# Small weight columns in sixteen parts behind later loads, and FoX's first keys ahead of GLA's first queries and keys

## What is computed

```
h = rms_norm(x, g_norm1) * (1.0 + scale1) + shift1
proj = h @ w_in                       # (256, 2048) @ (2048, 16416)
(gq, gk, gv, gg, ga_low, fq, fk, fv, f_logit, gate_a, gate_b) = split(proj)
log_a = log_sigmoid(ga_low @ w_gla_a_up + b_gla_a) / GLA_TAU   # ga_low: 16 columns
log_f = log_sigmoid(f_logit + b_fox_f)                         # f_logit: 16 columns
```

## Time and profile before

| | |
|---|---|
| median of three runs | 1872.38 us (1868.65 to 1874.75) |
| the profiled execution | 1868.97 us |
| its span, first to last instruction | 1867.2 us |
| TensorE busy | 1825.2 us (98%) |
| VectorE / ScalarE busy | 1251.1 us (67%) / 852.0 us (46%) |
| mean granted TensorE clock | 0.994 |
| moved by DMA | 445.71 MB, mean 239 GB/s |

### The profile page before, as it was taken

The page is one execution under the profiler, slowest core; times in us unless marked ns, Lnnn a source line. Parts: engine busy times, 40 slices in busy tenths (PEclk is TensorE's granted clock), DMA queues, the critical chain, the costliest instruction groups (busy, mean ns, idle before and its releaser), DMA issues.

```text
span 1867.2 us, 21786 instructions
## 1 busy us (share of the span) xinstructions
PE 1825.2 (98%) x8353; PEld 1482.5 (79%) x8353; DVE 1251.1 (67%) x1402; ACT 852.0 (46%) x1089; POOL 21.2 (1%) x44
## 2 busy tenths in 40 slices
PE   6998999999999999999999999999999999999998
PEld 3666888888888888888887788788888888888886
DVE  5997667676666667667666787876555555555555
ACT  4444555455544544334433455443444344434443
POOL 1000000000000000000000000000000000000000
PEclk9999999999999999999999999999999999999999
DMA  9998898899987987999989786687665666666663
GB/s 383 401 320 256 217 225 280 244 238 254 210 211 241 214 240 242 254 263 323 323 241 272 258 284 217 220 277 230 193 188 181 197 190 188 188 195 191 182 191 125
DMA packets 216944, 445.71 MB, mean 239 GB/s; under 512 B 18565, under 2 KB 35045, under 8 KB 216458
## 3 DMA queue, kind: packets, MB, share of 16 engines
q1 hardware_dynamic: 215448, 440.77, 78.7%
q10 hardware_dynamic: 1138, 3.50, 0.5%
q0 software_dynamic: 256, 0.05, 0.0%
HBM read 442.12 MB, written 2.10 MB: 238 GB/s over the span
## 4 chain that ended last, share of the span: by engine, by line
PE 81%; DMA 6%; DVE 3%; issue 2%; ACT 1%; SPq 1%; POOLq 0%; POOL 0%; DVEq 0%; ACTq 0%
PE ps L1815 75%; DMA raw<-in_w_in 4%; DMA raw<-in_w_proj_fox 1%; PE ps L1799 1%; ACT whi L714 1%; DVE wlo L1193 1%; DMA raw<-in_w_proj_gla 1%; DVE acc L1311 1%; PE ps L1919 1%; SPq L597 0%; DVE acch L1165 0%; PE ps L1971 0%; PE ps L1725 0%; PE ps L1928 0%; PE ps L1723 0%
## 5 line engine op out<-in xcount | busy, mean ns | idle before, releaser
L1193 DVE TENSOR_TENSOR wlo<-raw,whi 128x1024 fp32r<-128x1024 f32 x604 | 738.1, 1224 | 559.5 <-ACT whi L714 557.4
L714 ACT ACTIVATE whi<-raw 128x1024 fp32r<-128x1024 f32 x604 | 639.4, 1060 | 917.7 <-PE ps L1815 663.6
L1815 PE MATMUL ps<-whi,hT 128*128 128x512 f32 x3264 | 1042.5, 395 | 7.9 <-DVE wlo L1193 7.6
L1815 PEld LDWEIGHTS ps<-whi,hT 128*128 128x128 f32 x3264 | 615.3, 189 | 154.8 <-DVE wlo L1193 16.7
L1815 PE MATMUL ps<-wlo,hT 128*128 128x512 f32 x1632 | 637.4, 391 | 0.0
L1815 PE MATMUL ps<-whi,oaT 128*128 128x512 f32 x1248 | 390.9, 392 | 0.0
L1815 PEld LDWEIGHTS ps<-wlo,hT 128*128 128x128 f32 x1632 | 308.0, 189 | 63.2 <-issue 1.9
L1815 PEld LDWEIGHTS ps<-whi,oaT 128*128 128x128 f32 x1248 | 234.4, 188 | 49.6 <-issue 1.2
L1815 PE MATMUL ps<-wlo,oaT 128*128 128x512 f32 x624 | 243.0, 389 | 0.0
L1311 DVE SCALAR_TENSOR_TENSOR acc<-raw,cond,acc 128x1024 f32<-128x1024 f32 x120 | 153.4, 1278 | 0.2
L1815 PEld LDWEIGHTS ps<-wlo,oaT 128*128 128x128 f32 x624 | 117.2, 188 | 25.1 <-issue 1.2
(11 more groups left out here) (245 smaller groups left out, 817.6 us busy)
## 6 DMA issues: line engine op xcount, KB each, us to landing
raw<-in_w_ff SPq DMA_DIRECT2D x264, 512.0 KB, 4.0
raw<-in_w_in SPq DMA_DIRECT2D x248, 512.0 KB, 7.0
raw<-in_w_ada SPq DMA_DIRECT2D x128, 512.0 KB, 5.8
first<-in_w_ada SPq DMA_DIRECT2D x64, 512.0 KB, 10.2
raw<-in_w_in SPq DMA_DIRECT2D x64, 256.0 KB, 6.2
raw<-in_w_proj_fox SPq DMA_DIRECT2D x32, 512.0 KB, 5.8
raw<-in_w_proj_gla SPq DMA_DIRECT2D x32, 512.0 KB, 5.6
raw<-in_w_out SPq DMA_DIRECT2D x32, 512.0 KB, 4.9
```

Of the source, the lines that this page charges most:

```text
L714: nc.scalar.activation(parts(g)[0][:], raw[POS_G[g] % RING][:], ACT.Copy).then_inc(s_hi, 1)
L1193: V.tensor_tensor(rest[:], raw[POS_G[g] % RING][:], top[:].bitcast(F32), ALU.subtract).then_inc(s_lo, 1)
L1815: i = T.matmul(ps[bank(name, t)][:], src[:, kt, hl, tk], w[:, k, :], start=(kt == 0 and n == 0), stop=(kt == KT - 1 and n == 2))
```

## The change

Four things are edited. The two sections behind HEAD change places: `fk0` has units 24 to 31, `qk0` units 32 to 39, and their stage, turn and take change places with them. The two small DMAs become sixteen: behind each of the loads at stream positions 30 to 37 stand two that bring 2 of the 16 row blocks (256 runs of 64 bytes, 16 KB, each). `small_hi` waits for all sixteen. And the chain of the small columns is written one to three steps later; `shift_sum` stays where it was.

```
-FOX = [("qk", 0), ("fk", 0), ("fv", 0)] + ...
+FOX = [("fk", 0), ("qk", 0), ("fv", 0)] + ...
+SMALL_FROM = G_FOX + 6
...
             for pos in range(loaded, len(STREAM)):
-                if pos == G_FOX + 4:
+                load(pos)
+                if SMALL_FROM <= pos < SMALL_FROM + UG:
                     sp.wait_ge(s_zero, 1)
-                    sp.dma_start(small[:, :, 0:RANK], w_in_v[:, :, C_LOW:C_LOW + RANK]).then_inc(s_small, 16)
-                    sp.dma_start(small[:, :, 32:32 + FH], w_in_v[:, :, C_FL:C_FL + FH]).then_inc(s_small, 16)
-                load(pos)
+                    ks = slice(KU * (pos - SMALL_FROM), KU * (pos - SMALL_FROM) + KU)
+                    sp.dma_start(small[:, ks, 0:RANK], w_in_v[:, ks, C_LOW:C_LOW + RANK]).then_inc(s_small, 16)
+                    sp.dma_start(small[:, ks, 32:32 + FH], w_in_v[:, ks, C_FL:C_FL + FH]).then_inc(s_small, 16)
...
-                act.wait_ge(s_small, 32)
+                act.wait_ge(s_small, 32 * UG)
```

ScalarE's steps (stage and take of `fk0` and `qk0` change places as well):

```
-                    if u == 8:
+                    if u == 11:
                         small_hi()
-                    if u == 12:
+                    if u == 14:
                         small_log()
-                    if u == 13:
+                    if u == 15:
                         decay_abs()
-                    if u == 14:
+                    if u == 16:
                         logs()
-                    if u == 21:
+                    if u == 22:
                         decay_evac()
```

More of the change, by code:

```diff
@@ L39 @@
 HEAD = [("gg", 0), ("gv", 0), ("fq", 0)]
-FOX = [("qk", 0), ("fk", 0), ("fv", 0)] + [(what, it) for it in range(1, 4) for what in ("fq", "fk", "fv")]
+FOX = [("fk", 0), ("qk", 0), ("fv", 0)] + [(what, it) for it in range(1, 4) for what in ("fq", "fk", "fv")]
 GLA = [(what, it) for it in range(1, 4) for what in ("qk", "gg", "gv")]
@@ L756, in fox_stage @@
                 if u == 8:
-                    stage(("fq", it) if it else ("qk", 0), fqk_tok)
+                    stage(("fq", it) if it else ("fk", 0), fqk_tok)
                 if u == 11:
@@ L762, in fox_stage @@
                     else:
+                        take_turned(("fk", 0), ((fk, 1.0),))
+                if u == 16:
+                    stage(("fk", it) if it else ("qk", 0), fqk_tok)
+                if u == 19:
+                    if it:
+                        take_turned(("fk", it), ((fk, 1.0),))
+                    else:
                         take_turned(("qk", 0), ((gq[0], GSC), (gk[0], 1.0)))
[L764 to L767, removed]
             def shift_silu(g):
@@ L1499, in _ @@
                     else:
-                        if u == 8:
+                        if u == 11:
                             small_lo()
-                        if u == 11:
+                        if u == 13:
                             small_join()
-                        if u == 13:
+                        if u == 15:
                             decay_min()
-                        if u == 14:
+                        if u == 16:
                             log_sigmoids()
-                        if u == 16:
+                        if u == 17:
                             forget_cols()
-                        if u == 18:
+                        if u == 19:
                             forget_cums()
@@ L2007, in _ @@
                     else:
-                        if u == 11:
+                        if u == 13:
                             small_cols()
-                        if u == 13:
+                        if u == 15:
                             decay_logits()
-                        if u == 16:
+                        if u == 17:
                             forget_turn()
-                        if u == 18:
+                        if u == 19:
                             forget_sums()
-                        if u == 20:
+                        if u == 21:
                             decay_sums()
@@ L2020, in _ @@
                     if u == 10:
-                        turn(("fq", it) if it else ("qk", 0), fqk_tok)
+                        turn(("fq", it) if it else ("fk", 0), fqk_tok)
                     if u == 18:
-                        turn(("fk", it), fqk_tok)
+                        turn(("fk", it) if it else ("qk", 0), fqk_tok)
                     if u < 8:
@@ L2026, in _ @@
                         if it or u >= FOX_EARLY:
-                            token_unit(("fq", it) if it else ("qk", 0), u, hT, ready)
+                            token_unit(("fq", it) if it else ("fk", 0), u, hT, ready)
                     elif u < 16:
-                        token_unit(("fk", it), u - 8, hT)
+                        token_unit(("fk", it) if it else ("qk", 0), u - 8, hT)
                     else:
```

## The result

| | before | after |
|---|---|---|
| median (lowest to highest) | 1870.52 us (1866.81 to 1874.75), 4 runs | 1885.38 us (1882.99 to 1888.3), 4 runs |
| profiled execution, its span | 1868.97, 1867.2 us | 1882.99, 1881.2 us |
| busy and idle time of TensorE in the span | 1825.2 and 42.0 us | 1832.0 and 49.2 us |
| mean granted clock | 0.994 | 0.991 |

The ratio is 1.008, with an interval from 1.0067 to 1.0093: the kernel after is 0.8% slower, 14.9 us by the medians. The forecast was 1879.6, in a range from 1871 to 1888.5. The sum worked out before was +7.2 us; the two profiled executions are 14.0 apart. 27 executions of the kernel before, timed beside e1 to e4, lie between 1865.87 and 1875.48 us, with granted clocks from 0.989 to 0.995, so a pair of single traces tells the size of an effect only to a few microseconds.

The account below looks back on a forecast made before the run. TensorE, busy 1825 of 1867 us, was taken as the bound. Front -3.5, second turn +3.5, `small_cols` +2.7, `forget_turn` +1.8 and `shift_sum` +2.7 made +7.2 on 1868.97: 1876.2, as a median 1879.6; range 1871 to 1888.5.

Parts of the forecast that it names:

- Front, -3.5 us: Up to the turn of `fq0`: earlier loads and no `wlo` waits put that turn at 155.4, 3.5 us won.
- Second turn, +3.5 us: Turn of units 24 to 31 at step 10: TensorE waits 3.5 us behind unit 35's load, the gain back at 0.
- `small_cols`, +2.7: At `small_cols`: `small_hi` stands behind `hi` of unit 38, so TensorE waits 2.7 us where before it had none.
- c: Time one `qk` load (two DMAs, 1 KB runs) takes in a non-empty queue: taken as 2.5 us, bounds 1.3 and 4.1.
- `forget_turn`, +1.8: At `forget_turn`: two units instead of three after `decay_logits` cover the chain, so TensorE waits 1.8 us.
- `shift_sum`, a wait of 3.2: At `shift_sum`: `decay_evac` at step 22 leaves no unit between, so the wait is 0.48 + 2.8, 2.7 us more.
- From 225 us on the two run parallel.: Rest of the kernel: from 225 us on the timelines of before and after run parallel.
- Fast `qk` loads: Rival, chance 0.34: `qk` loads take below 2.3 us, the rings recover, supply waits shrink; sum -0.2 to +5.5 us.
- The chain is covered: Rival, 0.08: ScalarE runs ahead, no waits at `shift_sum` and `forget_turn`, the whole 5.3 us come through; median 1867 to 1870.
- A fixed time per part: Rival, chance 0.04: each pair of parts costs the queue 4 us instead of 1, 9 us more at the turn; median 1889.
- The slow landings are the queue's own pace: Rival, 0.04: landings at 146 to 157 us are not from SP's hold, the 3.5 us stay away; sum +10.7, median 1883.

Follow-up runs that it names:

- e1: The kernel before with the sixteen small-column DMAs alone, old section order and old steps: 1866.26 us, ratio 0.9976 to before.
- e4: The kernel before with only the two sections swapped, small columns whole and old steps: 1870.88 us, ratio 1.0004 to before.
- e10: The kernel after with each `qk0` unit one DMA of 2 KB runs, other columns in place of the keys: 1873.28 us, ratio 1.0016 to before.
- e3: The kernel before with only the chain's twelve steps moved as in the change: 1877.74 us, ratio 1.0041 to before.
- e6: The kernel after with fourteen extra matmuls, results unused, ahead of `shift_sum`: 1881.97 us, ratio 1.0054 to before.
- e7: e1 with `stage` of `fq0` ahead of the conversion of unit 32: 1864.38 us, ratio 0.9964 to before.
- e9: e1 with the small columns in 32 DMAs of 8 KB in place of 16 of 16 KB: 1866.38 us, ratio 0.9971 to before.
- e2: The kernel after with the chain of the small columns at its old steps: 1869.49 us, ratio 0.9996 to before.
- e8: The kernel after with `small_hi` and `small_lo` back at step 8: 1880.85 us, ratio 1.0054 to before.
- e5: The kernel after with `shift_sum` one step later, 23 instead of 22: 1878.11 us, ratio 1.0035 to before.

## Why the prediction held, and where it did not

The sign and the places of the waits were right; the size came out 6.8 us short, +14.0 in the spans for a sum of +7.2. Point by point:

1. **Front, -3.5 us.** 1.1 us of it came, and the half clock from 157.0 us on took more than that back. The turn of `fq0` ran at 157.74, not at 155.4. SP issued unit 32's load at 148.78 (148.3 worked out), so the step that failed is the landing: 5.5 us taken, 7.4 measured, within the 3.8 to 8.8 of the earlier trace rows; as one DMA with runs of 2 KB the same load took 4.7 (e10, 149.30 to 154.01). The `wlo` waits at 149 and 153 us fell from 2.4 to 0.8. That after has 3.2 us in five places is mostly another thing, which neither edit sets: at unit 27 it waits 1.4 us where before was at half clock from 137.1 us on and came too late to wait. In all thirteen traces one of the two is there and never both: the wait in seven (after, e1, e3, e4, e6, e7, e9), the half level just ahead of it in six. e1 shows that the front's gain exists, 3.9 us, as long as unit 32 is an FK load with runs of 2 KB and not a `qk` one.
2. **Second turn, +3.5 us.** It waits, 0.84 us. Unit 35 was converted at 168.1, not 165.6; from unit 32 to 35 it was 12.0 us, against 11.8 worked out. That agreement is luck: by the packets' times a `qk` load took some 3 us and not 2.5, and a pair of parts 0.35 and not 1.0, and over three of each the two errors cancel. The wait is short because TensorE came late itself: its first turn was 2.3 us later, and it ran at half clock behind it. In e2 the wait was 2.16.
3. **`small_cols`, +2.7.** 4.57 us. From unit 35 to 38 it took 12.4 us and not 10.1: with 2.6 for w3 and a1 as in the sum, c was 3.3 there. Between 32 and 35 it was 2.6 with the pairs at 1.0 (12.0 less 3.0 and 1.3, by three) and 3.2 with them at 0.35. c = 2.5 was too low, inside its bounds of 1.3 and 4.1; here no pair stood in the queue to make up for it.
4. **`forget_turn`, +1.8.** 1.64 us, in after and in e3. **`shift_sum`, a wait of 3.2.** 3.20 us, in both. These two rested on order alone and came out within 0.2 us.
5. **Nothing for the clock.** This is the missing term. All waits had been priced at their own length. Ahead of `shift_sum` after has four stretches at half clock from 157 us on, 17.0 us, and one at 88.7; before has two, at 106.3 and 137.1 (both have the head's first besides). That made 6.9 us of busy time. Two of the four lie at waits of 3.44 and 4.57 us, one begins 1.8 us behind the wait of 1.64, and one has no wait ahead of it. The stretch behind the wait of 3.20 us is not in the 6.9; before has one at a wait of 2.34 us at 1171.6, which after has not at the same wait of 2.35, so in the spans they cancel.
6. **"From 225 us on the two run parallel."** From 234.85 on after is 2.8 us shorter, so what is lost early is not kept whole: waits that before has near 1010 to 1030 us are smaller in a kernel that comes later.

That the idle time of the whole span rose by 7.2 us, the very sum, is an accident: it is 9.9 ahead of `shift_sum` and -2.8 behind it, from terms that each came out otherwise but for those of point 4. The median fell into the range because the range left room for a c of up to 3.8, and the clock took that room.

The rivals. *Fast `qk` loads*: refuted in after by the rows above; e10 is what it would have been, and its median stands 2.5 us above before, in that rival's -0.2 to +5.5. *The chain is covered*: refuted by the waits of 1.64 and 3.20. *A fixed time per part*: refuted by e9, for ten more DMAs ahead of unit 32 made its turn 1.4 us later and no more, and SP's issue of that unit's load was 1.7 us later. The Trainium skill, "DMA: Bandwidth & Descriptors", in "Anatomy of one DMA", says of DMAs on the GpSimd path that their fixed cost is mostly the latency of completion; these go through SP, and that run agrees. *The slow landings are the queue's own pace*: its number, 1883, was the nearest, and its front was what happened, but by another cause; e1 shows that taking SP's hold away does win time.

What is shown: the steps cost 7.5 us alone (e3), the late `small_hi` 4.9 in after (e8, good to some 4 us), the wait at `shift_sum` 8.4 with what follows it (e5, to some 3.5), the 1 KB loads 12 (e10, to some 3). They are not additive; each was taken out of after by itself, and 25 us by that count stand against a loss of 15.

## What to carry to other kernels

When steps of a chain are moved, work out for each engine what now stands between a producer and its reader; those terms need no price of a DMA, and they were the ones that came out right. Price a wait of an engine that is otherwise never idle at more than its length, and look at the granted clock of the stretches behind waits in the trace of before. Before a section is brought forward, look at the shape of its loads: a load of the same bytes in shorter runs is a slower one, and whatever is queued behind it on every engine is late with it.

## What the runs showed of the hardware

- **Half clock at short waits, not at every one.** In after the granted clock fell to 1.2 GHz at waits of 3.44 and 4.57 us, 0.6 us behind the end of one of 3.20 and 1.8 us behind the end of one of 1.64; each microsecond there holds half the work. Between 100 and 270 us the thirteen traces have 13 waits of TensorE of 3.2 us or more, and the half level stands at or within a microsecond behind every one. Of their 24 waits from 1.1 to 2.9 us it follows 6, within 2 us. The same wait of 1.6 us at `forget_turn` was followed by it in after and e3 and not in e5, e6, e8 and e10, and the longest without it is before's 2.87 us. What decides among the shorter ones is not shown.
- **Half clock without a wait.** The stretch from 201.3 us has no wait ahead of it. The decay logits' matmuls had run there, 3.69 us of a kind that uses 17 rows, and in nine of the thirteen traces the half level begins during them or within 1.1 us of their end. The kernel before has the same matmuls, of the same length, and stays at the full clock (after, then before):

```profile
197.26 3.69 PE L1872 MATMUL ps<-wup,gl 17*128 17x512 f32 x8
```

```profile
182.69 3.69 PE L1867 MATMUL ps<-wup,gl 17*128 17x512 f32 x8
```

- **Runs of 1 KB against 2 KB**: 1.4 to 1.7 us more for 512 KB, at DMA engines shown as busy throughout in both. The Trainium skill, "DMA: Bandwidth & Descriptors", in "Specifications", asks for 512 bytes or more for line rate. Both kinds are above that and by it neither should lose; the trace shows that the shorter one does. Its packets took 92 ns on average against 93 to 106 for twice the bytes (e10's section). The slow and fast phases of the earlier trace rows show in the same way: packets of 1 KB took 95 ns on average from 505 to 560 us and 55 from 600 to 660. What makes the slow packets slow no run shows.
- **What an issue costs SP does not follow its runs.** Most parts held SP for 0.43 to 0.47 us, with 256 runs or with 128. Of the two whole DMAs, with 2048 runs each, the first took 1.35 us and the second 8.77 before, and 0.46 and 6.70 in e4. So the long hold is no price of the runs alone; what the second waits for in the queue is not shown.
